# Attention scores of a hybrid decoder block from stacked high and low halves, in fp32r products instead of fp32

## The chip, the core and the metric

The kernel runs on one core of a Trainium2 chip. The time is device time in microseconds (us) of one execution; the profile is one execution of its own, with its own time. TensorE multiplies (PE in the rows, PEld its weight loads), VectorE is DVE, ScalarE is ACT, GpSimd is POOL, and SP is the queue that issues the weight transfers.

## What is computed

A block with 256 tokens and width 1024: an mLSTM mixer and a dense SwiGLU, then attention with three branches (compressed, selected, window) over shared keys and values, then a top-2-of-8 expert SwiGLU, and a last norm. The change touches the scores of the three branches. Sixteen heads of width 64 share four groups of keys. With 256 tokens all four selection blocks are always taken and the window holds everything, so the selected and the window branch differ only in their keys and values.

```python
# cut from nsa_mixer: g groups, r heads in a group
s_c = jnp.einsum('bgrqd,bgcd->bgrqc', qb, k_cmp) * scale - sl5 * dist_c      # 15 compressed keys
p_cmp = safe_softmax(jnp.where(dist_c >= 0, s_c, -jnp.inf))
o_cmp = jnp.einsum('bgrqc,bgcd->bgrqd', p_cmp, v_cmp)
s_s = jnp.einsum('bgrqd,bgqnkd->bgrqnk', qb, ks) * scale - sl6 * dist_s      # selected blocks
o_slc = jnp.einsum('bgrqk,bgqkd->bgrqd', safe_softmax(s_s), vs)
s_w = jnp.einsum('bgrqd,bgkd->bgrqk', qb, kw) * scale - sl5 * dist_w         # window
o_win = jnp.einsum('bgrqk,bgkd->bgrqd', safe_softmax(s_w), vw)
return gb[..., 0:1] * o_cmp + gb[..., 1:2] * o_slc + gb[..., 2:3] * o_win
```

## The kernel before

Five engine programs run side by side, each written out by hand in its own order, and wait for each other through semaphores. There is no scheduler: the order in the code is the order of the work.

**Weights.** All weights come in slots of 1 MB. SP loads them into a ring of 7 (`raw`), each when the slot seven before it has been used (`s_used`). ScalarE rounds a slot to fp32r (`w_hi`, L433), VectorE subtracts (`w_lo`, L853), and TensorE multiplies high by high, low by high and high by low (`mm3`, L1475 to L1477). `split_to(m)` makes the halves up to slot m, on ScalarE and on VectorE; `AHEAD` is 3 slots.

**Ahead of the attention** (about 340 to 407 us). Four slots give the compressed inputs and the two sets of keys: `kt` holds keys with the width of 64 on the rows, twice (rows 0 to 63 and 64 to 127), ScalarE copying the lower groups (L594, L595) and VectorE the upper ones (L1075, L1076). Four slots, with the compression between them, give the queries: bank i holds four heads, and one copy of ScalarE scales and stores it in `qt` (`q_copied`, L604), two heads above each other: even heads on rows 0 to 63, odd ones on rows 64 to 127. The compressed keys go to `kc` in a block form, so that one product serves two heads (L624), and the compressed values to `vbd` (L627), both by ScalarE.

**Attention** (about 407 to 500 us). There are 32 steps, one for a head and a token tile of 128. `ORDER` lists the tile and the group: eight heads of tile 1, eight of tile 0, eight of tile 1, eight of tile 0. A head of tile 1 sees 256 keys in each of two branches, so its score has 512 columns; one of tile 0 sees 128, and has 256. The two are called wide and narrow below. Step n on TensorE is the score of head n+3 (`head_scores`, L1823), one part of the value products of an earlier group (`group_part`, L1849, L1851), and the transposes of head n (`head_transpose`, L1833). Score and value products and transposes are fp32. VectorE adds the position bias to a score out of one of three banks and takes the maximum (L1130, L1134), ScalarE makes the exponentials (L648), VectorE turns the sums into coefficients (L1141, L1142), both scale a half (L675, L1146), TensorE transposes, and ScalarE copies the result for the value products (L656). The compressed scores (`cmp_scores`, L1805) of one tile stand before the loop and those of the other in steps 5 and 6. The first three scores, the first compressed scores and the products of the first value slot stand before the loop, and those of the second value slot follow steps 0 and 1.

**Behind it** come the output projection and the experts, 336 more slots.

These lines of TensorE's program are the ones that the change replaces:

```python
def cmp_scores(t, pairs):
    for pair in pairs:
        ins = mm(B[7][:, pair * 64:pair * 64 + 48], qt[:, pair, cmp_tile(t) * P:(cmp_tile(t) + 1) * P],
                 kc[:, 2 * pair // R, :], start=True, stop=True)
...
    mm(B[n % 3][:, 0:2 * lk], qt[lo:lo + 64, h // 2, t * P:(t + 1) * P], kt[lo:lo + 64, :, h // R, 0:lk],
       start=True, stop=True).then_inc(s_as, 1)
```

## Time and profile before

| | us |
|---|---|
| median of 3 runs | 1437.31 |
| lowest and highest | 1434.43, 1438.07 |
| the profiled execution | 1439.59 |
| its span in the profile | 1437.8 |
| busy in the span: PE, DVE, ACT, POOL | 1391.2, 1184.5, 1022.9, 43.8 |

The profile's page gives the busy time of each engine and, in 40 slices, their shares. The span is the time from the first to the last instruction; the 1.8 us between it and the execution's time lie around it. A matmul's duration in the rows is longer than its distance to the next, since matmuls are pipelined: what one costs is read from start to start, or from the chain of waits, where pieces do not overlap. One fp32 matmul of the program stands as two records in the trace, one fp32r matmul as one. Inputs of type fp32r are printed as f32 as well.

### The profile page before, as it was taken

To read this page: it belongs to the slowest core of one execution; us is meant where nothing else is said; L and a number is where in the kernel's file an instruction comes from. 1 tells how busy PE (TensorE), PEld (TensorE's weight loads), DVE (VectorE), ACT (ScalarE), POOL (GpSimd) and SP (SyncE) were. 2 spreads that over 40 slices of the span, in tenths; PEclk is the share of its full clock that TensorE was granted. 3 is DMA by queue.
4 is the path that set the end of the run, shared out by engine and by line. 5 is a ranking of instruction groups with operands and counts; after the bars stand their busy time and mean duration, and the time that the engine had idled before them with its cause. 6 is when DMAs were issued, how large, how long until landed. Compare 5 with 4: busy or idle time off the path is not lost.

```text
span 1437.8 us, 19005 instructions
## 1 busy us (share of the span) xinstructions
PE 1391.2 (97%) x6962; PEld 1142.7 (79%) x6962; DVE 1184.5 (82%) x1091; ACT 1022.9 (71%) x1066; POOL 43.8 (3%) x98
## 2 busy tenths in 40 slices
PE   7999999999999989999999999999999999999996
PEld 7987888888974578788888878888878888878774
DVE  6846654547768679899999999999999999999997
ACT  5546644435567747788888788887878887887875
POOL 7000000001000010000000000000000000000000
PEclk9999999999999989999999999999999999999999
DMA  7543555554630129899999999999999999999985
GB/s 307 177 162 131 192 189 178 176 203 147 235 118 1 39 94 350 326 394 416 407 399 402 399 391 402 411 395 403 398 388 398 408 409 395 391 401 398 415 353 214
DMA packets 59707, 431.68 MB, mean 300 GB/s; under 512 B 6624, under 2 KB 6624, under 8 KB 7520
## 3 DMA queue, kind: packets, MB, share of 16 engines
q1 hardware_dynamic: 59472, 429.95, 76.8%
q8 instruction: 56, 0.92, 0.2%
q10 hardware_dynamic: 144, 0.52, 0.1%
q14 instruction: 35, 0.29, 0.1%
HBM read 429.40 MB, written 1.05 MB: 299 GB/s over the span
## 4 chain that ended last, share of the span: by engine, by line
PE 89%; DVE 4%; DMA 3%; ACT 2%; issue 1%; POOL 0%; SPq 0%; DVEq 0%; POOLq 0%; ACTq 0%
PE bank L1475 19%; PE bank L1477 19%; PE bank L1476 19%; PE bank L1946 6%; PE bank L1947 6%; PE bank L2008 3%; PE bank L1965 3%; PE bank L1966 3%; DMA raw<-in_moe 3%; PE bank L1823 2%; PE bank L1849 2%; DVE w_lo L1352 1%; PE bank L1917 1%; PE bank L1833 1%; PE bank L1995 1%
## 5 line engine op out<-in xcount | busy, mean ns | idle before, releaser
L1352 DVE TENSOR_TENSOR w_lo<-raw,w_hi 128x2048 fp32r<-128x2048 f32 x332 | 750.6, 2289 | 46.7 <-ACT w_hi L748 44.0
L748 ACT ACTIVATE w_hi<-raw 128x2048 fp32r<-128x2048 f32 x332 | 632.9, 1919 | 137.5 <-DMA raw<-in_moe 58.7
L1475 PE MATMUL bank<-w_hi,ht_hi 128*128 128x512 f32 (+1 forms) x768 | 299.3, 390 | 0.9 <-DVE ht_lo L885 0.9
L1477 PE MATMUL bank<-w_hi,ht_lo 128*128 128x512 f32 (+1 forms) x768 | 296.2, 386 | 0.0
L1476 PE MATMUL bank<-w_lo,ht_hi 128*128 128x512 f32 (+1 forms) x768 | 295.9, 385 | 0.0
L853 DVE TENSOR_TENSOR w_lo<-raw,w_hi 128x2048 fp32r<-128x2048 f32 x73 | 166.6, 2290 | 109.7 <-ACT w_hi L433 109.6
L433 ACT ACTIVATE w_hi<-raw 128x2048 fp32r<-128x2048 f32 x74 | 141.4, 1918 | 96.4 <-PE bank L1477 92.8
L1946 PE MATMUL bank<-w_hi,ht_hi 128*128 128x512 f32 x448 | 177.5, 396 | 1.4 <-DVE w_lo L1352 1.4
L1947 PE MATMUL bank<-w_lo,ht_hi 128*128 128x512 f32 x448 | 174.8, 390 | 0.0
L1475 PEld LDWEIGHTS bank<-w_hi,ht_hi 128*128 128x128 f32 x768 | 144.4, 188 | 29.6 <-issue 1.4
L1477 PEld LDWEIGHTS bank<-w_hi,ht_lo 128*128 128x128 f32 x768 | 144.3, 188 | 29.4
L1476 PEld LDWEIGHTS bank<-w_lo,ht_hi 128*128 128x128 f32 x768 | 144.4, 188 | 28.2
L1475 PE MATMUL bank<-w_hi,at_hi 128*128 128x512 f32 x312 | 122.8, 393 | 2.5 <-DVE w_lo L1352 2.5
L1476 PE MATMUL bank<-w_lo,at_hi 128*128 128x512 f32 x312 | 121.5, 389 | 0.0
L1477 PE MATMUL bank<-w_hi,at_lo 128*128 128x512 f32 x312 | 121.5, 389 | 0.0
L1946 PEld LDWEIGHTS bank<-w_hi,ht_hi 128*128 128x128 f32 x448 | 84.2, 188 | 20.2 <-DVE w_lo L1352 3.1
L1947 PEld LDWEIGHTS bank<-w_lo,ht_hi 128*128 128x128 f32 x448 | 84.2, 188 | 16.9
L1965 PE MATMUL bank<-w_hi,at_b 128*128 128x512 f32 x224 | 91.5, 408 | 3.2 <-DVE w_lo L1352 3.1
L1966 PE MATMUL bank<-w_lo,at_b 128*128 128x512 f32 x224 | 88.7, 396 | 0.0
L1475 PEld LDWEIGHTS bank<-w_hi,at_hi 128*128 128x128 f32 x312 | 58.6, 188 | 17.2 <-DVE w_lo L1352 5.5
L1477 PEld LDWEIGHTS bank<-w_hi,at_lo 128*128 128x128 f32 x312 | 58.6, 188 | 12.3
L1476 PEld LDWEIGHTS bank<-w_lo,at_hi 128*128 128x128 f32 x312 | 58.6, 188 | 11.8
(328 smaller groups left out, 1671.1 us busy)
## 6 DMA issues: line engine op xcount, KB each, us to landing
raw<-in_moe SPq DMA_DIRECT2D x336, 1024.0 KB, 7.8
raw<-in_wts SPq DMA_DIRECT2D x71, 1024.0 KB, 4.9
xs<-in_x SPq DMA_DIRECT2D x2, 512.0 KB, 4.0
out<-xn SPq DMA_DIRECT2D x2, 512.0 KB, 2.6
pk<-in_packed SPq DMA_DIRECT2D x1, 517.0 KB, 5.9
g1b<-in_norm_ffn ACTq DMA_DIRECT2D x1, 512.0 KB, 3.8
gfb<-in_norm_final SPq DMA_DIRECT2D x1, 512.0 KB, 12.0
```

Of the source, the lines that this page charges most:

```text
L433: a(w_hi[:, n % SPLIT, :], raw[:, n % RAW, :], ACT.Copy).then_inc(s_hi, 1)
L748: a(w_hi[:, n % SPLIT, :], raw[:, n % RAW, :], ACT.Copy).then_inc(s_hi, 1)
L853: v.tensor_tensor(w_lo[:, n % RAW, :], raw[:, n % RAW, :], w_hi[:, n % SPLIT, :].bitcast(F32), ALU.subtract).then_inc(s_lo, 1)
L1352: v.tensor_tensor(w_lo[:, n % RAW, :], raw[:, n % RAW, :], w_hi[:, n % SPLIT, :].bitcast(F32), ALU.subtract).then_inc(s_lo, 1)
L1475: mm(out_, sh, mh, start=first, stop=False)
L1476: mm(out_, sh, ml, start=False, stop=False)
L1477: return mm(out_, sl, mh, start=False, stop=last)
L1946: mm(bank[:, :], both, weights(w_hi, n, 512)[:, k, :], start=kk == 0, stop=False)
L1947: ins = mm(bank[:, :], both, weights(w_lo, n, 512)[:, k, :], start=False, stop=kk == 7)
L1965: mm(B[2 + half][:, :], at_b[:, block], weights(w_hi, n, 1024)[:, k, w], start=first, stop=False)
L1966: ins = mm(B[2 + half][:, :], at_b[:, block], weights(w_lo, n, 1024)[:, k, w], start=False, stop=last)
L2008: ins = mm(B[4 + c % 2][:, to:to + CAP_B], src[:, c % 2, j * P:(j + 1) * P], fold[:], start=True, stop=True)
```

## The change

The queries are kept as a high half, rounded to fp32r, and a low half, what the rounding leaves, stacked on the 128 rows: for each head the high half on rows 0 to 63 and the low half on rows 64 to 127 (`q_first` for heads 0 to 7, `q_last` for heads 8 to 15, where `ct` was). The keys' high half `kt_hi` stands twice, as `kt` did, and a product over 128 rows is then (high + low query) times high key. A second and a third product over rows 0 to 63 add the high query times the low key, for each of the two branches (`kt_lo`, eight small tiles in free places). All are fp32r. The compressed scores are built likewise from `kc_hi` and `kc_lo`, for each head instead of each pair.

ScalarE copies each query bank in two halves, and three small copies replace the two of `kc`, two of them to fill a sixteenth column. VectorE makes the low halves of the keys (8 subtractions), of the queries (8) and of the compressed keys (1). GpSimd no longer clears `kc`. The odd buffer of transposed weights (`pt_odd`) and `fold` move to other places.

```diff
@@ ScalarE
-            a(qt[:, 2 * i:2 * i + 2, :], B[i % 2][:, :].rearrange("p (b t) -> p b t", b=2), ACT.Copy,
-              scale=DB ** -0.5).then_inc(s_qc, 1)
+            for odd in range(2):
+                a(queries(i, odd, slice(0, 64)), B[i % 2][64 * odd:64 * odd + 64, :].rearrange("p (b t) -> p b t", b=2), ACT.Copy,
+                  scale=DB ** -0.5).then_inc(s_qc, 1)
...
-        for odd in range(2):
-            rows_ = slice(64 * odd, 64 * odd + 64)
-            a(kc[rows_, :, 32 * odd:32 * odd + NC_], B[5][rows_, 0:G * NC_].rearrange("p (g n) -> p g n", g=G),
-              ACT.Copy).then_inc(s_kc, 1)
+        a(kc_hi[:, :, 0:NC_], B[5][:, 0:G * NC_].rearrange("p (g n) -> p g n", g=G), ACT.Copy).then_inc(s_kc, 1)
+        spare = B[5][:, 0:G].rearrange("p (g o) -> p g o", o=1)
+        a(kc_hi[:, :, NC_:16], spare, ACT.Copy).then_inc(s_kc, 1)
+        a(kc_lo[0:64, :, NC_:16], spare[0:64], ACT.Copy).then_inc(s_kc, 1)
@@ VectorE
+                dve.wait_ge(s_kva, 2 * i + 2)
+                dve.wait_ge(s_kvd, 2 * i + 2)
+                for g in range(G):
+                    rows_ = slice(64 * (g % 2), 64 * (g % 2) + 64)
+                    v.tensor_tensor(kt_lo[i - 2][g][0:64, :], B[4 + i % 2][rows_, (g // 2) * T:(g // 2 + 1) * T],
+                                    kt_hi[rows_, i - 2, g, :].bitcast(F32), ALU.subtract).then_inc(s_kl, 1)
...
+        def q_low(i):
+            for odd in range(2):
+                dve.wait_ge(s_qc, 2 * i + odd + 1)
+                v.scalar_tensor_tensor(queries(i, odd, slice(64, 128)),
+                                       B[i % 2][64 * odd:64 * odd + 64, :].rearrange("p (b t) -> p b t", b=2), DB ** -0.5,
+                                       queries(i, odd, slice(0, 64)).bitcast(F32), ALU.mult, ALU.subtract).then_inc(s_ql, 1)
+
+        for i in range(2):
+            split_to(Q_SLOT[i] + AHEAD)
+            q_low(i)
         split_to(Q_SLOT[2] + AHEAD)
+        q_low(2)
...
+        q_low(3)
+        dve.wait_ge(s_kc, 3)
+        v.tensor_tensor(kc_lo[0:64, :, 0:NC_], B[5][0:64, 0:G * NC_].rearrange("p (g n) -> p g n", g=G),
+                        kc_hi[0:64, :, 0:NC_].bitcast(F32), ALU.subtract).then_inc(s_kcl, 1)
         split_to(BO0 + 1)
@@ TensorE
+            tile = slice(cmp_tile(t) * P, (cmp_tile(t) + 1) * P)
+            for h in heads:
+                to = B[7][:, h * 32:h * 32 + 16]
+                mm(to, query(h)[:, tile], kc_hi[:, h // R, :], start=True, stop=False)
+                ins = mm(to, query(h)[0:64, tile], kc_lo[0:64, h // R, :], start=False, stop=True)
...
-            mm(B[n % 3][:, 0:2 * lk], qt[lo:lo + 64, h // 2, t * P:(t + 1) * P], kt[lo:lo + 64, :, h // R, 0:lk],
-               start=True, stop=True).then_inc(s_as, 1)
+            mm(B[n % 3][:, 0:2 * lk], query(h)[:, tile], kt_hi[:, :, g, 0:lk], start=True, stop=False)
+            for b in range(2):
+                ins = mm(B[n % 3][:, b * lk:(b + 1) * lk], query(h)[0:64, tile], kt_lo[b][g][0:64, 0:lk],
+                         start=False, stop=b == 1)
+            ins.then_inc(s_as, 1)
```

On TensorE, in step 5 of the attention, stand before: the narrow score of head 8, a part of the value products, four pairs of compressed scores and the transposes of head 5.

```order
L1823 MATMUL bank<-kt,qt 128x256
L1849 MATMUL bank<-pt_even,vv 64x512
L1851 MATMUL bank<-pct,vbd 64x128
L1805 MATMUL bank<-kc,qt 128x48 x4
L1833 MATMUL bank<-ident,sc 128x128 x4
```

The same step now; the lines L1848 and L1849 stand eight times each, in turn, of which two pairs are shown at the start.

```order
L1866 MATMUL bank<-kt_hi,q_first 128x256
L1868 MATMUL bank<-kt_lo_113,q_first 128x128
L1868 MATMUL bank<-kt_lo_117,q_first 128x128
L1895 MATMUL bank<-pt_even,vv 64x512
L1897 MATMUL bank<-pct,vbd 64x128
L1848 MATMUL bank<-kc_hi,q_first 128x16
L1849 MATMUL bank<-kc_lo,q_first 128x16
```

One score became three products and the four pairs of compressed scores 16; the transposes (now L1879) still end the step.

On VectorE, from the last splits ahead of the attention to the first bias, stood the gates and then the splits of slots 67 and 68.

```order
L1085 TENSOR_TENSOR gat<-bank,pk 128x2x24 x2
L1091 TENSOR_SCALAR gat<-gat 128x96
L1092 RECIPROCAL gat<-gat 128x96
```

Now the low halves of the last two query banks stand on both sides of the gates, and that of the compressed keys behind them.

```order
L1106 SCALAR_TENSOR_TENSOR q_last<-bank,q_last 64x2x256 x2
L1118 TENSOR_TENSOR gat<-bank,pk 128x2x24 x2
L1124 TENSOR_SCALAR gat<-gat 128x96
L1125 RECIPROCAL gat<-gat 128x96
L1106 SCALAR_TENSOR_TENSOR q_last<-bank,q_last 64x2x256 x2
L1128 TENSOR_TENSOR kc_lo<-bank,kc_hi 64x4x15
```

The splits of slots 67 and 68 follow behind these rows, where before they followed the reciprocal.

## Rows read from the trace of the kernel before

**Rows 1.** PE, PEld, DVE, ACT, POOL busy, PEclk, DMA share, GB/s; page's DMA

```profile
451.00:470.00 19.00, 19.00 (x67) 7.88 (x68) 16.29 (x42) 16.19 (x53) 0.00 (x0) 1.00 0.00 1
522.00:532.00 10.00, 4.69 (x21) 4.24 (x20) 8.83 (x36) 5.70 (x5) 3.06 (x2) 0.52 0.16 67
...
DMA  7543555554630129899999999999999999999985
```

**Rows 2.** Chain of waits in the attention loop: start and length in us

```profile
427.73 0.59 PE bank L1833 x4
432.24 1.02 PE bank L1805 x8
441.69 0.63 PE bank L1823 x2
456.28 1.05 PE bank L1823 x2
```

**Rows 3.** Timeline of DVE: first bias, narrow and wide coefficients

```profile
411.00 0.68 DVE L1130 SCALAR_TENSOR_TENSOR sc<-dat,bank 128x512 f32<-128x512 f32 x1
446.71 0.17 DVE L1141 RECIPROCAL coef<-att 128x2 f32<-128x2 f32 x1
448.31 0.17 DVE L1141 RECIPROCAL coef<-att 128x2 f32<-128x2 f32 x1
463.70 0.17 DVE L1141 RECIPROCAL coef<-att 128x2 f32<-128x2 f32 x1
465.69 0.16 DVE L1141 RECIPROCAL coef<-att 128x2 f32<-128x2 f32 x1
```

**Rows 4.** Timeline of PE: neighbouring fp32r products, 512 and 16 or 8 columns

```profile
330.25 0.39 PE L1477 MATMUL bank<-w_hi,at_lo 128*128 128x512 f32 x1
330.48 0.39 PE L1475 MATMUL bank<-w_hi,at_hi 128*128 128x512 f32 x1
...
519.49 0.26 PE L1899 MATMUL bank<-ws_hi,ht_hi 128*128 128x16 f32 x1
519.60 0.25 PE L1900 MATMUL bank<-ws_hi,ht_lo 128*128 128x8 f32 x1
```

**Rows 5.** Timeline of PE: transposes, 24 fp32r products between, a score

```profile
421.65 0.66 PE L1833 MATMUL bank<-ident,sc 128*128 128x128 f32 x4
...
424.97 1.12 PE L1823 MATMUL bank<-kt,qt 64*128 64x512 f32 x2
```

**Rows 6.** Timeline of PE: first three scores, and the fourth

```profile
406.88 1.98 PE L1823 MATMUL bank<-kt,qt 64*128 64x512 f32 x6 [2.12 <-ACT vbd L627]
...
416.22 1.12 PE L1823 MATMUL bank<-kt,qt 64*128 64x512 f32 x2
```

**Rows 7.** Group of DVE, a query copy of ACT, DVE's waits 352 to 412

```profile
L1153 DVE TENSOR_TENSOR ht_lo<-bank,ht_hi 64x256 fp32r<-64x256 f32 x12 | 4.9, 412 | 1.0 <-ACT ht_hi L664 0.8
...
377.02 0.60 ACT L604 ACTIVATE qt<-bank 128x512 f32<-128x512 f32 x1 [3.35 <-PE bank L1477]
...
DVE w_lo L853 <- ACT w_hi L433: 16.0, 8, 5.2
```

**Rows 8.** Waits 427 to 492: us in total, times, longest

```profile
DVE sc L1130 <- PE bank L1823: 2.9, 5, 0.9
DVE coef L1141 <- ACT sc L648: 1.7, 7, 0.4
DVE pc L1101 <- PE bank L1805: 1.4, 1, 1.4
```

**Rows 9.** ACT and PE: scaling and transposes of heads 20 and 31

```profile
466.31 0.50 ACT L675 ACTIVATE sc<-sc,coef 128x256 f32<-128x256 f32 x1
...
469.13 0.66 PE L1833 MATMUL bank<-ident,sc 128*128 128x128 f32 x4
...
490.87 0.40 ACT L675 ACTIVATE sc<-sc,coef 128x128 f32<-128x128 f32 x1 [0.17 <-DVE coef L1142]
...
491.63 0.44 PE L1833 MATMUL bank<-ident,sc 128*128 128x128 f32 x2
```

More of the change, by code:

```diff
@@ L153, in trunk @@
     assert KD * T * 8 <= (28 + 4) * P * 4
+    ptg = [sb("pt_even", [P, 4, R, P], F32, sg_at)[0], sb("pt_odd", [P, 4, R, P], F32, hk_at + KD * T * 4)[0]]
+    q_last, _ = sb("q_last", [P, 8, T], FR, ct_at)
+    kt_lo = [[sb(f"kt_lo{b}{g}", [P, T], FR, at)[0] for g, at in enumerate(row)]
+             for b, row in enumerate(([xn_at + 4096 + 1024 * g for g in range(4)],
+                                      [sel_at, tri_at, pk_at + 1856, pk_at + 2880]))]
     iot, _ = sb("iot", [P, NE])
@@ L240, in head, with query, queries @@
         return t, R * g + n % R
+    def query(h):
+        return (q_first, q_last)[h // 8][:, h % 8, :]
+    def queries(i, odd, rows):
+        first = 4 * (i % 2) + odd
+        return (q_first, q_last)[i // 2][rows, first:first + 3:2, :]
     def cmp_tile(i):
@@ L1800, in values, with cmp_scores @@
                 ins.then_inc(s_used, 1)
[L1802 to L1807 removed]
+        def cmp_scores(t, heads):
+            tile = slice(cmp_tile(t) * P, (cmp_tile(t) + 1) * P)
[3 more added lines that the diff above has]
+                ins = mm(to, query(h)[0:64, tile], kc_lo[0:64, h // R, :], start=False, stop=True)
+            if heads[-1] == HB - 1:
                 ins.then_inc(s_cs, 1)
```

47 lines of the change are left out of this document (23 added, 24 removed).

## Prediction

> **What bounds the kernel now.** I read the stretches first: between 451 and 470 us, in the middle of the attention, TensorE is busy 19.00 of 19.00 us while VectorE is busy 16.29 and ScalarE 16.19 [rows 1]. TensorE is the bound, but the other two are only 14% below it, so a large saving on TensorE cannot all reach the end. The page's row of DMA tenths [rows 1] says what follows: in the attention the queues are nearly idle (the digits 0, 1, 2), since the ring of 7 weight slots is full, and from the 16th slice on they are full. Loads start again when TensorE frees slots behind the attention, so an earlier end of the attention moves the whole expert part by as much, neither more nor less.
>
> Then the chain of waits, for what a score costs inside the loop: 1.05 us for a head of the later token tile (512 columns, "wide"), 0.63 us for one of the first tile (256 columns, "narrow"), 1.02 us for four pairs of compressed scores [rows 2]. Then VectorE: one wide head takes it 1.99 us (463.70 to 465.69), a narrow one 1.60 us (446.71 to 448.31), both stretches without a wait [rows 3].
>
> **TensorE's part, step by step.** What an fp32r product costs from start to start: with 512 columns 0.23 us, with 16 or 8 columns still 0.11 us [rows 4]. With 256 columns and between fp32 neighbours I take it from a block of 24 such products: from the four transposes at 421.65 to the score at 424.97 are 3.32 us [rows 5], and four transposes before an fp32 score take 0.59 [rows 2], so the block costs 2.73, or 0.114 us each, with what the change from fp32 to fp32r and back costs inside it.
> - Wide score: 0.23 + 2 x 0.114 = 0.46 in place of 1.05, saves 0.59. There are 13 in the loop: 7.7 us.
> - Narrow score: one product of 256 columns and two of 128. No row shows fp32r with 128 columns. Below lies the price of 16 columns (0.11), above that of an fp32 score of 256 columns in two records, 0.63 / 2 = 0.31. I take 0.114, since rows on both sides of 128 columns (16 and 256) show it. 3 x 0.114 = 0.34 in place of 0.63, saves 0.28. There are 16: 4.5 us. At the upper end each would cost 0.74, 0.11 more than now, and the 4.5 saved become 1.8 lost.
> - The first three scores stand together before the loop and take 1.98 us [rows 6], not 3 x 1.05 = 3.15: even heads lie on rows 0 to 63, odd ones on 64 to 127, and two of them overlap. Now 3 x 0.46 = 1.37, saves 0.6.
> - Compressed scores: 8 products of fp32 become 32 of fp32r for each tile. 32 x 0.112 = 3.6 us; now 1.9 before the loop (9.34 us from 406.88 to 416.22, less 1.98 and less 48 x 0.114 for the values [rows 6]) and 2 x 1.02 inside it [rows 2]. Costs 1.7 + 1.55 = 3.3 us.
> TensorE's sum: 7.7 + 4.5 + 0.6 - 3.3 = 9.5 us less work.
>
> A page of the Trainium skill speaks against the change here: "TensorEngine Tiling (Array Packing)", section When to Use Tiling, advises two row tiles where the contraction is 64 deep, and the new score fills all 128 rows. The trace agrees where scores stand together (1.98 us) and only there; in the loop a transpose stands between any two. By that rule all scores of before would count half, the saving would be gone, and TensorE's work would rise.
>
> **Ahead of the attention.** VectorE gets 8 subtractions of 64x256 for the keys at 0.41 us (the same form in the attention [rows 7]), 8 of 64x512 for the queries at up to 0.69 (by the biased score, 512 elements read from a bank [rows 3]) and a small one: 3.3 + 5.5 + 0.3 = 9.1 us. In 352 to 412 us it waits 16.0 us for ScalarE's high halves [rows 7], and these additions fall between those waits; w_lo of a slot is made about one slot ahead of its use. Cost 0; if that cover were gone, at most 9.1. ScalarE copies each query bank in two halves, so 0.60 more for each of four [rows 7]; it waits for TensorE before each. Behind the last, one more small copy stands in front of the vbd copies, for which TensorE waits 2.12 us before its first score [rows 6]. Its price lies between 0 and 0.60 (a copy of 512 columns); I take 0.25, as it has 4 to 60 columns. TensorE's added waits (for the low halves of keys and queries) stand before products 10 us and more behind them; the one for kc_lo is met while ScalarE still copies vbd. The split of slot 67 moves behind the queries, and slot 68 is still the last thing before VectorE's first bias at 411.00 [rows 3].
>
> **What becomes late next.** The opening gets no faster: 0.25 later, 0.6 saved, 1.7 more for the compressed scores, so the fourth score, 416.22 now [rows 6], starts at about 417.6, and wins it back only over the next three heads. At the two heads with compressed scores TensorE again needs 1.55 us more and saves 0.6; the compressed bias, which waited 1.4 us for it [rows 8], comes some 0.45 us later.
>
> From there to the end VectorE and ScalarE set the pace. The 8 wide scores of the second half lie in 451 to 470: TensorE's 19.00 us become 19.00 - 8 x 0.59 = 14.3, under the 16.29 of VectorE and the 16.19 of ScalarE [rows 1]. In the middle TensorE trails: the scaling of head 20 starts at 466.31 and takes 0.50, its transposes start at 469.13, 2.3 us behind readiness [rows 9]. But for the last head this slack is almost gone: scaled at 490.87 + 0.40 = 491.27, transposed at 491.63, 0.36 us [rows 9]. The loop ends earlier by that 0.36 and by what the chain of VectorE and ScalarE gains itself. It gains its waits for TensorE: 2.9 us for scores from 427 us on, and of the 1.7 us for the exponentials some part, as ScalarE waited for transposes in its turn [rows 8]; I take half, 0.85. Sum: 0.36 + 2.9 + 0.85 - 0.45 - 0.25 = **3.4 us**. Of 9.5 us saved on TensorE 6.1 become waits. Lower end: the 0.85 is 0 and every second of the five waits is replaced by one for ScalarE: 1.5. Upper end: all 1.7, and the compressed bias not late: 4.7; I say 5. Behind the loop nothing changes.
>
> The profiled execution took 1439.59 us (span 1437.8), 2.3 above the median of the runs, 1437.31. It would come to 1436.2, the median to 1433.9.
>
> **Rivals.**
> - *TensorE's saving arrives whole.* Then the last transposes would not be held by their scaling, and the time is 1437.3 - 9.5 = 1427.8. For it: TensorE is 100% busy and trails by 2.3 us in the middle. Against: 0.36 us at the last head [rows 9], 16.29 of 19.00 on VectorE.
> - *Nothing arrives.* Short fp32r products are dear: at the upper end for 128 columns TensorE saves 9.5 - 16 x 0.39 = 3.3 us, and the narrow heads, for which VectorE needs only 1.60 us [rows 3] and TensorE sets the pace, take back what the wide ones give: about 0, 1437. Against: no row shows a short fp32r product over 0.12 us at full clock [rows 4].
> - *Slower: the clock falls inside the loop.* TensorE would now stop at nearly every head. In 522 to 532 it was busy 4.69 of 10 us and its granted clock was 0.52 [rows 1], so near the 1.2 GHz level and not the 2.4. Ten microseconds at half clock in the loop make 9 us of work into 18; less some 4 us of slack and with the gain of 3.4 given back in part, about +5: 1442. [...] Against: even with 6.1 us of new waits in 80 TensorE stays over 90% busy, and in 451 to 470 the clock is 1.00 [rows 1]. The Trainium skill's page "TensorE: Matmul & The Clock Gate", section What's actually happening, has the throttled state as the default that activity releases; that is this rival's rule, and the row of 522 to 532 agrees with it.
>
> **How the numbers follow.** A measurement of this kernel tells about 0.3%, 4.3 us, from no change. Forecast 0.57 (1432.3 to 1435.8; about a fifth of it gains over 4.3), whole saving or most of it 0.17, nothing arrives 0.16, clock or a lost cover ahead of the attention 0.10. Faster by over 0.3%: 0.17 + 0.12 = 0.29; slower 0.10; within 0.3%: 0.61. The range leaves out the outer half of the whole saving and of the slower case: 1429 to 1440.
>
> **What would show it.** In the profile of the changed kernel a wide score should be three products in 0.46 us, a narrow one in 0.34, and the compressed scores 16 times 0.11 in a row. VectorE's wait for scores should be nearly gone from 427 us on, TensorE should show idle before the transposes of some 6 us in sum, ended by ScalarE's or VectorE's scaling, and the last transposes should start 3 us earlier against the first score. Ahead of the attention no product should wait for w_lo, xc_lo or the new low halves. I am wrong if narrow scores take over 0.5 us, if TensorE still shows no idle time in the loop (then the first rival holds), if VectorE's heads become longer than 1.99 and 1.60 us, or if the granted clock in the loop falls below 1.00.

## The result and the profile after

The changed kernel takes 1452.06 us (median of 4 runs, 1449.89 to 1454.80) beside 1436.94 for the kernel before: a ratio of 1.0103, 95% interval 1.0087 to 1.0118. It is slower by 15.1 us, where 1433.9 and a range of 1429 to 1440 were forecast. Its profiled execution has a span of 1453.0 us.

First the stretches of the changed kernel. The columns are start and end, length, then busy time (and instructions) of PE, PEld, DVE, ACT and POOL, the granted clock of TensorE, the DMA share and GB/s:

```profile
407.00:411.00 4.00, 2.19 (x8) 1.19 (x8) 3.38 (x4) 3.60 (x8) 0.00 (x0) 1.00 0.61 244
411.00:421.00 10.00, 10.00 (x35) 9.13 (x34) 7.04 (x13) 4.08 (x14) 0.00 (x0) 0.53 0.00 1
421.00:425.00 4.00, 4.00 (x19) 3.98 (x20) 0.00 (x0) 0.00 (x0) 0.00 (x0) 0.50 0.00 0
425.00:444.00 19.00, 18.42 (x130) 15.46 (x129) 12.60 (x34) 10.21 (x30) 0.00 (x0) 0.99 0.33 111
444.00:447.00 3.00, 3.00 (x14) 2.72 (x15) 1.54 (x6) 1.25 (x5) 0.00 (x0) 0.80 0.00 0
447.00:459.00 12.00, 12.00 (x36) 8.73 (x37) 3.51 (x11) 3.61 (x13) 0.00 (x0) 0.50 0.01 1
462.00:509.00 47.00, 46.39 (x215) 25.58 (x212) 41.14 (x126) 41.94 (x147) 0.00 (x0) 1.00 0.00 1
```

Where the kernel before had the full clock without a break from 402 to 516 us (the stretch of rows 1 is a piece of that), this one falls to the 1.2 GHz level twice, over 411 to 425 and over 447 to 459 us. In both TensorE is listed as busy for all of the time. From 447 to 459 us VectorE and ScalarE have little to do: 3.51 and 3.61 us of work in 12.

What TensorE does at the two falls, from its timeline (start, length, line, output and inputs with rows x columns, count). L1866 and L1868 are the new score's high and low products, L1848 and L1849 those of the compressed scores, L1512 to L1514 the value projection, L1895 and L1897 a part of the value products, L1879 the transposes of a head (a transpose stands as one record):

```profile
408.81 0.50 PE L1866 MATMUL bank<-kt_hi,q_first 128*128 128x512 f32 x1 [1.86 <-ACT vbd L642]
409.24 0.50 PE L1868 MATMUL bank<-kt_lo,q_first 64*128 64x256 f32 x2
...
411.39 0.28 PE L1848 MATMUL bank<-kc_hi,q_first 128*128 128x16 f32 x1
411.60 0.32 PE L1849 MATMUL bank<-kc_lo,q_first 64*128 64x16 f32 x1
411.85 0.38 PE L1848 MATMUL bank<-kc_hi,q_first 128*128 128x16 f32 x1
...
413.08 0.38 PE L1848 MATMUL bank<-kc_hi,q_first 128*128 128x16 f32 x1
413.39 0.38 PE L1849 MATMUL bank<-kc_lo,q_first 64*128 64x16 f32 x1
...
421.14 0.58 PE L1512 MATMUL bank<-w_hi,hk_hi 128*128 128x256 f32 x1
...
421.52 0.41 PE L1513 MATMUL bank<-w_lo,hk_hi 128*128 128x256 f32 x1
421.74 0.41 PE L1514 MATMUL bank<-w_hi,hk_lo 128*128 128x256 f32 x1
...
428.66 0.40 PE L1866 MATMUL bank<-kt_hi,q_first 128*128 128x512 f32 x1
428.98 0.50 PE L1868 MATMUL bank<-kt_lo,q_first 64*128 64x256 f32 x2
429.42 0.66 PE L1879 MATMUL bank<-ident,sc 128*128 128x128 f32 x4
```

and at the first head with compressed scores in the loop:

```profile
443.23 0.28 PE L1848 MATMUL bank<-kc_hi,q_first 128*128 128x16 f32 x1
443.44 0.27 PE L1849 MATMUL bank<-kc_lo,q_first 64*128 64x16 f32 x1
443.64 0.28 PE L1848 MATMUL bank<-kc_hi,q_first 128*128 128x16 f32 x1
...
446.84 1.11 PE L1879 MATMUL bank<-ident,sc 128*128 128x128 f32 x4
```

A product of 16 columns starts 0.205 us after the one before it at full clock (443.23, 443.44, 443.64), and 0.31 at half clock (413.08, 413.39). The forecast had 0.112. The 32 of the first tile take from 411.39 to 421.14, 9.75 us, where 3.6 were forecast. Behind them the value projection runs at some 0.21 per product (421.52, 421.74) for another 4 us, twice its price at full clock, and the fourth score starts at 428.66, where the kernel before had it at 416.22 [rows 6].

The 32 products of the first tile lengthen the stretch at half clock, but they did not begin it. The first of them starts at 411.39, and the clock is down a third of a microsecond later, when one or two of them have run:

```profile
411.50:411.75 0.25, 0.25 (x2) 0.23 (x2) 0.25 (x1) 0.00 (x0) 0.00 (x0) 0.87 0.00 0
```

What stands in front are TensorE's stop of 1.86 us and 2.58 us of the new scores. The experiments come back to this.

The effect on the other engines, from the waits in 430 to 492 us (total, times, longest):

```profile
DVE sc L1167 <- PE bank L1868: 16.5, 5, 11.2
DVE pc L1138 <- PE bank L1849: 6.4, 1, 6.4
```

These are VectorE's waits for scores and for compressed scores, 2.9 and 1.4 us before [rows 8].

To place the 15 us I cut the attention at the transposes of heads 0, 8 and 31, in this and in all later kernels. Times in us; "clock" is where the granted clock was under 0.9 between 402 and 516 us, in steps of 3 us.

| kernel | first score to head 0 | heads 0 to 8 | heads 8 to 31 | span | clock under 0.9 |
|---|---|---|---|---|---|
| before | 10.39 | 23.98 | 50.38 | 1437.8 | nowhere |
| changed | 20.61 | 32.75 | 46.22 | 1453.0 | 411-426, 444-459 |
| low_rows128_compressed | 17.33 | 25.87 | 46.22 | 1438.8 | 411-423, 444-450 |
| low_rows128_all | 15.98 | 31.47 | 45.82 | 1444.5 | 408-420, 435-456 |
| compressed_fp32 | 17.42 | 24.25 | 46.23 | 1440.5 | 411-423 |
| compressed_one_product | 14.02 | 22.51 | 46.38 | 1431.2 | 408-417 |
| compressed_one_spread | 12.50 | 22.61 | 46.79 | 1431.8 | 408-414 |
| one_product_rows128_low | 12.42 | 25.12 | 46.76 | 1434.6 | 408-417, 432-441 |
| one_spread_rows128_low | 11.01 | 21.85 | 47.17 | 1432.3 | 411-414 |
| one_spread_scores_first | 10.90 | 22.62 | 46.79 | 1428.8 | nowhere |
| after_wide_columns | 27.17 | 38.77 | 48.47 | 1464.3 | 411-432, 456-480 |

The changed kernel is 10.2 us longer ahead of head 0, 8.8 longer over heads 0 to 8, and 4.2 shorter over heads 8 to 31. So the loop's gain is there, where the compressed scores are done, and both losses lie in the two stretches that hold the compressed scores. Its first score starts 1.9 us later than before (408.81 against 406.88), but the products ahead of any changed instruction are 2.2 us later already, and in the kernels below (one_spread_scores_first apart, where this code is changed) the start of the first score varies between 406.7 and 410.0 with nearly the same code in front of it. So it is not laid to the change. What follows head 31 takes 940.5 to 946.2 us in all the traces, so a sum of one trace holds to some 3 us.

### The profile page after: what moved, and what is told of

The parts are those of the page before. It is cut to its first block, busy times and chain, and to the rows that moved or that the text cites. A ratio compares the mean times of both kernels' runs of the same rounds, so it can differ in the third digit from the quotient of the medians.

```text
span 1453.0 us, 19158 instructions
## 1 busy us (share of the span) xinstructions
PE 1406.0 (97%) x7026; PEld 1165.6 (80%) x7026; DVE 1192.6 (82%) x1108; ACT 1023.0 (70%) x1071; POOL 43.7 (3%) x97
## 3 DMA queue, kind: packets, MB, share of 16 engines
HBM read 429.40 MB, written 1.05 MB: 296 GB/s over the span
## 4 chain that ended last, share of the span: by engine, by line
PE 88%; DVE 5%; ACT 2%; DMA 2%; issue 1%; POOL 0%; SPq 0%; DVEq 0%; POOLq 0%; ACTq 0%
PE bank L1512 19%; PE bank L1514 19%; PE bank L1513 19%; PE bank L1993 6%; PE bank L1994 6%; PE bank L2012 3%; PE bank L2013 3%; PE bank L2055 3%; DMA raw<-in_moe 2%; DVE w_lo L1389 2%; PE bank L1895 1%; PE bank L1964 1%; PE bank L1879 1%; PE bank L2042 1%; PE bank L1868 1%
## 5 line engine op out<-in xcount | busy, mean ns | idle before, releaser
L1512 PE MATMUL bank<-w_hi,ht_hi 128*128 128x512 f32 (+1 forms) x768 | 299.4, 390 | 1.1 <-DVE ht_lo L900 0.9
L1514 PE MATMUL bank<-w_hi,ht_lo 128*128 128x512 f32 (+1 forms) x768 | 296.3, 386 | 0.0
L1512 PEld LDWEIGHTS bank<-w_hi,ht_hi 128*128 128x128 f32 x768 | 144.4, 188 | 29.9 <-issue 1.4
L1514 PEld LDWEIGHTS bank<-w_hi,ht_lo 128*128 128x128 f32 x768 | 144.3, 188 | 29.5
L1512 PE MATMUL bank<-w_hi,at_hi 128*128 128x512 f32 x312 | 122.8, 394 | 3.0 <-DVE w_lo L1389 3.0
L1514 PE MATMUL bank<-w_hi,at_lo 128*128 128x512 f32 x312 | 121.5, 389 | 0.0
L1512 PEld LDWEIGHTS bank<-w_hi,at_hi 128*128 128x128 f32 x312 | 58.5, 188 | 17.9 <-DVE w_lo L1389 6.2
L1514 PEld LDWEIGHTS bank<-w_hi,at_lo 128*128 128x128 f32 x312 | 58.6, 188 | 12.4
```

The lines of the kernel that those rows point to most:

```text
L1512: mm(out_, sh, mh, start=first, stop=False)
L1514: return mm(out_, sl, mh, start=False, stop=last)
```

## Experiments

Three theories stood after this, and the expectations go by their letters. **A**: changing between products over 128 and over 64 rows costs TensorE about 0.09 us at each change, and this is the loss. **B**: an fp32r product of 16 columns costs 0.2 us whatever its rows. **C**: the clock falls because the products have few columns, whatever rows they use, and that is most of the loss.

### Taking the change of rows out

low_rows128_compressed: the compressed low-key product uses all 128 rows.

```
...
-        v.tensor_tensor(kc_lo[0:64, :, 0:NC_], B[5][0:64, 0:G * NC_]...
+        v.tensor_tensor(kc_lo[:, :, 0:NC_], B[5][:, 0:G * NC_]...
...
-                ins = mm(to, query(h)[0:64, tile], kc_lo[0:64, h // R, :], start=False, stop=True)
+                ins = mm(to, query(h)[:, tile], kc_lo[:, h // R, :], start=False, stop=True)
```

> The changed kernel with one edit: the second product of each compressed score runs over all 128 rows (the compressed keys' low half stands twice, so it also adds low query times low key) instead of rows 0 to 63. The count of products stays 32 for each tile. Theory A (a product pays its weight load in the open when its rows differ from those of the one before): start to start of the compressed products falls from 0.205 us at full clock (0.31 at half) to 0.11, so the 32 before the loop take 3.6 us instead of 9.8, and the time comes down by some 10 to 12 us, to 1440 to 1442. Rival B (a 16-column fp32r product costs 0.2 us whatever its rows): distance and time stay as in the changed kernel, 1452. Rival C (the clock falls because the products have few columns, and that is most of the loss): the distance falls to 0.11 but the clock still falls behind 411 us, and the time is 1446 or more.

low_rows128_all: the same, and the attention's low-key products too (the low keys are written to rows 64 to 127 as well, 8 more subtractions).

```
+                    for half in range(2):
+                        v.tensor_tensor(kt_lo[i - 2][g][64 * half:64 * half + 64, :], ...
...
-                ins = mm(B[n % 3][:, b * lk:(b + 1) * lk], query(h)[0:64, tile], kt_lo[b][g][0:64, 0:lk],
+                ins = mm(B[n % 3][:, b * lk:(b + 1) * lk], query(h)[:, tile], kt_lo[b][g][:, 0:lk],
```

> As low_rows128_compressed, and the two low-key products of each attention score run over 128 rows too; for that VectorE makes each of the eight low key tiles on both halves, 8 more subtractions of 0.41 us ahead of the attention. Theory A: a wide score with the transposes behind it comes down from 1.24 to about 1.05 us on TensorE, a narrow one from 0.85 to 0.65, some 6 us less work on TensorE in the loop, of which perhaps 3 arrive, since the last heads already wait for their scaling: 1437 to 1439. Rival B: no difference to low_rows128_compressed. If the added VectorE work ahead of the attention is on the path, products ahead of 409 us wait for w_lo and the time is longer by up to 3 us.

Measured: 1442.01 us (4 runs, ratio to before 1.0043, 1.0027 to 1.0060) and 1446.13 (4 runs, 1.0068, 1.0051 to 1.0084). Timeline of TensorE in the first:

```profile
410.57 0.26 PE L1849 MATMUL bank<-kc_lo,q_first 128*128 128x16 f32 x1
410.68 0.26 PE L1848 MATMUL bank<-kc_hi,q_first 128*128 128x16 f32 x1
```

and in the second:

```profile
408.32 0.40 PE L1869 MATMUL bank<-kt_lo,q_first 128*128 128x256 f32 x2
408.56 0.39 PE L1867 MATMUL bank<-kt_hi,q_first 128*128 128x512 f32 x1
408.79 0.39 PE L1869 MATMUL bank<-kt_lo,q_first 128*128 128x256 f32 x2
```

The compressed products are back at 0.11 us, and a wide score at 0.46 to 0.47 (408.32 to 408.79), the two prices of the forecast. So the change of rows is what they lacked, and B is out: it takes a pair of compressed products from 0.22 to 0.41 and a wide score from 0.46 to 0.86. Each product of a pair starts some 0.205 us behind the other, the one over 64 rows like the one over 128, so the price lies in the change in either direction and not in the 64 rows. Of the 15.1 us, 10.0 come back with the first edit by the medians (8.6 by the ratios to the kernel before). Its time is at the upper end of what A gave it, and the clock still falls, as C had it, though the time stays under C's 1446.

The second edit missed its expectation of 1437 to 1439 by 7 us. With less work on TensorE in the loop the clock stays down from 438 to 453 us, and the kernel takes 4.1 us more than the first (1445.57 to 1448.31 against 1440.57 to 1445.39). Granted clock of low_rows128_all, same columns as above, and a product just behind a stop of TensorE:

```profile
420.00:435.00 15.00, 14.34 (x120) 13.92 (x120) 9.87 (x26) 6.91 (x20) 0.00 (x0) 1.00 0.39 137
438.00:453.00 15.00, 15.00 (x57) 11.34 (x55) 5.76 (x20) 5.36 (x19) 0.00 (x0) 0.50 0.00 1
...
436.33 1.58 PE L1896 MATMUL bank<-pt_even,vv 128*64 128x512 f32 x2 [1.05 <-ACT pt_even L671]
```

TensorE had stopped for 0.66 us up to 434.34 and for 1.05 up to 436.33. The two value products behind the second stop are partly slow already (1.58 us; two take 1.07 at full clock), and the first compressed product of the loop starts only at 438.28. Here the clock fell right behind the stops, ahead of the compressed products.

In the opening, too, the clock of this kernel is down before its first compressed product starts:

```profile
409.25:409.50 0.25, 0.25 (x3) 0.25 (x2) 0.07 (x1) 0.25 (x1) 0.00 (x0) 0.79 0.08 33
...
409.53 0.21 PE L1849 MATMUL bank<-kc_hi,q_first 128*128 128x16 f32 x1
```

### 32 products added to the kernel before

The kernel before with 32 added fp32r products, whose results nobody reads, ahead of its own compressed scores; rows and columns varied.

```
+        for j in range(32):
+            r_ = slice(0, 64 if j % 2 else P)     # or slice(0, P)
+            mm(B[7][:, 0:16], hk_hi[r_, j % KD, 0:P], hk_lo[r_, j % KD, 0:16], start=True, stop=True)
         cmp_scores(0, range(HB // 2))
```

> The kernel before with 32 added fp32r products of 16 columns ahead of the first compressed scores; they go to a bank that is written anew behind them, and alternate between 128 and 64 rows. It measures the disputed product by itself, 128 columns of stationary, 16 columns moving. Theory A: 0.205 us each at full clock, 6.6 us in sum if the clock holds. Rival B: the same here and in before_32_full_rows. Rival C: the clock falls during or behind them here and in before_32_full_rows.

> As before_32_alternating, but all 32 added products have 128 rows. Theory A: 0.11 us each, 3.6 us in sum, clock 1.00. Rival B: 0.2 us each. Rival C: the clock falls in spite of the shorter run.

> before_32_full_rows with 256 columns in each of the 32 added products instead of 16. By start to start they should cost the same, 0.11 us each, 3.7 us. If it is the few columns that let the clock fall behind 413 us, it stays at 1.00 here and the time is about 3.7 above before, 1440. If any such burst behind the idle time before the scores does it, the clock falls as there, to 0.50 for some 7 us.

> The kernel before with 32 added fp32r products of 256 columns ahead of the compressed scores, over 128 and 64 rows in turn: the fourth of a table of two by two (16 or 256 columns, all rows or alternating). If both few columns and the alternation let the clock fall, each by itself, it falls to 0.50 here as in after_wide_columns, the 32 take 0.205 us each at first and 0.255 at half clock (7 to 8 us), and the time is 1437 + 7.5 + 3 to 6 = 1447 to 1451. If the fall in after_wide_columns came from the scores in front of the products (fp32r, also alternating) and not from the products, the clock holds at 1.00 here: 6.6 us for the 32, and 1443 to 1445.

One run each. Per product is start to start at full clock; the fall is the first 3-us window under 0.9:

| | time, us | per product | clock |
|---|---|---|---|
| 16 columns, all rows | 1441.66 | 0.112 | falls in 414-417, back at 423 |
| 16 columns, rows alternating | 1448.42 | 0.206 | falls in 411-414, back at 423 |
| 256 columns, all rows | 1443.64 | 0.123 | 1.00 throughout |
| 256 columns, rows alternating | 1454.2 | 0.315 | falls in 414-417, back at 432 |

The prices come from the timeline of TensorE, a group's length less the last record over the count less one. In before_32_alternating:

```profile
408.94 1.30 PE L1862 MATMUL bank<-hk_lo,hk_hi 128*128 128x16 f32 x6
```

and in before_32_alternating_wide:

```profile
411.64 1.64 PE L1862 MATMUL bank<-hk_lo,hk_hi 128*128 128x256 f32 x5
```

that is (1.30 - 0.27) / 5 = 0.206 and (1.64 - 0.38) / 4 = 0.315. The stretch 414 to 417 us of before_32_full_rows (columns as above):

```profile
414.00:417.00 3.00, 3.00 (x16) 3.00 (x16) 2.82 (x9) 2.02 (x8) 0.00 (x0) 0.52 0.00 0
```

of before_32_wide_columns:

```profile
414.00:417.00 3.00, 3.00 (x29) 3.00 (x28) 2.90 (x7) 1.82 (x6) 0.00 (x0) 1.00 0.00 0
```

and of before_32_alternating_wide:

```profile
414.00:417.00 3.00, 3.00 (x7) 1.73 (x7) 2.82 (x9) 2.02 (x9) 0.00 (x0) 0.53 0.00 0
```

Theory A's price is confirmed in the other kernel, and on the clock each theory had half. In these four traces the clock fell behind 16 columns on all rows, where A expected 1.00, and behind 256 columns with the rows changing, and did not fall behind 256 columns on all rows. All four stretches show TensorE fully busy in the profile, so the busy share doesn't tell them apart. The last was forecast too low (0.205 to 0.255 us a product, and 1447 to 1451 in all), and so was the time of the third (1440). The last was run because the next experiment had come out against its expectation.

Two limits belong to this table. Each row is one trace, and in all four the added products stand behind the same stop of TensorE (2.13 us) and the same old scores; no such row was run without the stop. And the fall comes 4 us and more behind the first added product (at about 413 where that starts at 408.94, at about 414 where it starts at 409.75 and 409.77), not a third of a microsecond as in the changed kernel.

after_wide_columns: the changed kernel, each compressed product over 256 columns of the score keys; it leaves out the compressed keys, so its compressed scores are not those of the block.

```
+                to = B[7][:, 0:256]
-                mm(to, query(h)[:, tile], kc_hi[:, h // R, :], start=True, stop=False)
-                ins = mm(to, query(h)[0:64, tile], kc_lo[0:64, h // R, :], start=False, stop=True)
+                mm(to, query(h)[:, tile], kt_hi[:, 0, h // R, 0:256], start=True, stop=False)
+                ins = mm(to, query(h)[0:64, tile], kt_lo[0][h // R][0:64, 0:256], start=False, stop=True)
```

> The changed kernel, with each of its 64 compressed products over 256 columns instead of 16: the score keys' halves (kt_hi, kt_lo of tile 0) stand in for the compressed keys, so the compressed scores and what is worked out from them are wrong; count and rows of the products (128 and 64 in turn) are those of the changed kernel. If it is the few columns of these products that let the granted clock fall, the clock holds at 1.00 through steps 5 and 6 and nearly so from 408 to 426 us, a pair of products still takes 0.41 to 0.43 us (the alternation), the stretch before the loop takes 6.6 to 7 us instead of 9.8, head 0 is transposed 6 to 7 us earlier than in the changed kernel, and the time is 1452 - 10 to 14 = 1438 to 1442. If the alternation of rows itself is what lets the clock fall, the clock is 0.50 over about 10 us as in the changed kernel and the time stays at 1450 to 1454.

It took 1466.11 us (4 runs, 1.0193, 1.0166 to 1.0219), 14 us more than the changed kernel, where 10 to 14 less were expected if few columns were the whole reason. Its timeline:

```profile
412.90 0.58 PE L1849 MATMUL bank<-kt_hi,q_first 128*128 128x256 f32 x1
413.41 0.58 PE L1850 MATMUL bank<-kt_lo,q_first 64*128 64x256 f32 x1
```

One product starts 0.51 us after another, with the rows changing and at half clock. The expectation was also wrong in the price of a change: it put a pair at 0.41 to 0.43, which is what two products of 16 columns take. A change costs more with longer products: 0.09 us with 16 columns, 0.19 with 256.

### Shorter compressed scores

compressed_one_product: the keys' high and low halves stand side by side, so one product of 32 columns on all 128 rows does a head, and VectorE adds the two halves of the result (one more step for each tile).

```
-    kc_hi, _ = sb("kc_hi", [P, G, 16], FR)
-    kc_lo, _ = sb("kc_lo", [P, G, 16], FR)
+    kc2, _ = sb("kc2", [P, G, 32], FR)
+    kc_hi, kc_lo = kc2[:, :, 0:16], kc2[:, :, 16:32]
...
+                ins = mm(to, query(h)[:, tile], kc2[:, h // R, :], start=True, stop=True)
...
+            step(v.tensor_tensor(p, both[:, :, 16:16 + NC_], p, ALU.add))
```

> low_rows128_compressed with the two products of a compressed score joined into one of 32 columns (high keys beside low keys, VectorE adds the two column sets, one more step of 0.4 us for each tile): 16 products for a tile in place of 32, all over 128 rows. Attention scores as in the changed kernel. Theory A with the clock as second cause (few columns in a row let the clock fall): before the loop 1.8 us of 32-column products in place of 3.6, so the clock either holds or falls for less long; at steps 5 and 6 0.9 us each, where it should hold. Time 1434 to 1438. If the clock falls as in low_rows128_compressed (0.50 for 8 to 10 us behind 411), the number of short products is not what decides, and the time is 1439 or more.

compressed_one_spread: the same 16 products of the first tile stand one by one behind three value products each, those of the second in five small pieces.

```
+                if i == 0:
+                    cmp_scores(0, (8 * t + k,))
...
-                cmp_scores(1, range(8 * (n - 5), 8 * (n - 5) + 8))
+                cmp_scores(1, range(4) if n == 5 else range(11, 14))
...
```

> compressed_one_product with the 16 products of the first tile spread among the value products (one behind each three of 256 columns) and those of the other tile in three pieces within steps 5 and 6. Same work, other order. If the clock falls because short products stand in a row, it holds here, at 1.00 from 405 to 500 us, and the time is 1431 to 1434, below before. If it falls as in compressed_one_product, the cause is the attention scores or the idle time before them, not the compressed products.

compressed_fp32: one fp32 product of 16 columns over the stacked halves, with the compressed keys kept in fp32 and no low half of them.

```
...
+                ins = mm(to, query(h)[:, tile].bitcast(F32), kc_hi[:, h // R, :], start=True, stop=True)
```

> The changed kernel's attention scores, but the compressed scores in fp32: one product for each head over the stacked halves, 16 columns, no low keys, no change of rows. 16 fp32 products for a tile, 32 records of 0.12 us as in the kernel before, so 3.8 us in place of 1.9 before and 9.8 in the change. It is the attention scores' half of the change, and its compressed part is 2 us dearer a tile than before. If few columns let the clock fall, whatever the type, it falls here as in low_rows128_compressed and the time is 1440 to 1443. If fp32r is what does it, the clock holds: 1435 to 1438.

Measured, 10 runs each: compressed_one_product 1433.05 (0.9976, 0.9965 to 0.9987), compressed_one_spread 1434.17 (0.9978, 0.9965 to 0.9992) and compressed_fp32 1440.81 (1.0023, 1.0011 to 1.0035). Stretches of compressed_one_product:

```profile
409.00:415.00 6.00, 6.00 (x30) 5.86 (x31) 5.83 (x10) 2.26 (x8) 0.00 (x0) 0.55 0.00 1
420.00:443.00 23.00, 22.42 (x143) 16.84 (x143) 19.07 (x55) 15.90 (x49) 0.00 (x0) 1.00 0.26 92
```

With the new attention scores untouched and only the compressed ones rewritten, 19.0 us come back against the changed kernel by the medians (18.2 by the ratios), and the result is below the kernel before. In the loop the clock holds. In the opening it still falls for a few microseconds, with 16 short products where there were 32. The fp32 form holds the clock in the loop too, where each half of its 16 products takes 1.96 us. In the opening the halves take 2.83 and 3.42 (411.62, 414.45 and 417.87 are their starts and their end), and the clock is down from 411 to 423: 7.0 us more than before from the first score to head 0. Its time is the one expected if the clock falls whatever the type. Spreading the products shortens the opening by 1.5 us in the trace and shows in no time (the two intervals coincide).

The spread kernel missed its expectation that the clock holds, and what was written for that case applies: the cause of the opening's fall is then "the attention scores or the idle time before them, not the compressed products". In all the kernels with the new scores and a stop of 1.8 us or more in front of them, the clock goes down 1.2 to 3.3 us behind the start of the first score. In the changed kernel, compressed_one_product and compressed_one_spread, which have the same stop and the same scores, it is 2.9 to 3.0 us in all three. What the form of the compressed scores sets there is how long the clock stays down: about 14, 7 and 3 us.

### Taking the change of rows out of the attention's scores as well

one_product_rows128_low and one_spread_rows128_low: the two kernels above with the attention's low-key product on all 128 rows (the diff of low_rows128_all).

> The kernel compressed_one_product, with the attention's low-key product over all 128 rows too, which takes the row change out of every score (8 more subtractions on VectorE ahead of the attention). If a row change costs 0.09 to 0.10 us at each side of a low-key product, a wide head saves 0.37 us and a narrow one 0.25 in TensorE's row (13 x 0.37 + 16 x 0.25 = 8.8), of which the loop, paced by VectorE and ScalarE at most heads, gives 1 to 3: 1430 to 1432. If the shorter scores let the granted clock fall in the loop, as they did in low_rows128_all (0.50 from 438 to 453 us), 5 or more are lost: 1436 to 1440.

> The kernel compressed_one_spread, with the attention's low-key product over all 128 rows. As one_product_rows128_low: 1430 to 1433 if only the row changes go; 1436 to 1440 if the clock falls. If the clock falls in one_product_rows128_low and not here, what lets it fall is the compressed products in a row, and the spread cures it; if it falls in both, the short scores themselves do.

Measured, 12 runs each: 1437.80 (1.0008, 0.9993 to 1.0023) and 1434.09 (0.9977, 0.9967 to 0.9987). The clock falls in the first, over 432 to 441 us, and not in the loop of the second. In the opening it falls in both, and in the second before its first compressed product starts:

```profile
411.00:412.00 1.00, 1.00 (x7) 0.92 (x7) 0.41 (x2) 0.90 (x1) 0.00 (x0) 0.61 0.04 16
...
412.38 0.23 PE L1853 MATMUL bank<-kc,q_first 128*128 128x32 f32 x1
```

Timeline of the first where it falls in the loop:

```profile
433.08 1.59 PE L1897 MATMUL bank<-pt_even,vv 128*64 128x512 f32 x2 [1.05 <-ACT pt_even L671]
...
435.02 1.89 PE L1851 MATMUL bank<-kc,q_first 128*128 128x32 f32 x8
```

TensorE had stopped for 0.78 and 1.05 us just before, where compressed_one_product with its longer scores has one stop of 0.58. The products at 433.08 are partly slow already (1.59 us where two take 1.07), so the fall came right behind the stops and not at the eight short products that follow. That corrects what the expectation offered: the spread did not simply cure a row of short products. Why the clock held in the spread kernel, whose stops are 0.78 and 1.04 us, isn't settled by this pair. One trace doesn't speak for every execution here: the 12 of one_product_rows128_low lie between 1432.30 us, with a mean granted clock of 0.988 over the whole kernel, and 1442.81 with 0.983.

The second kernel answers what the cheaper scores are worth where the clock holds. TensorE's work over heads 8 to 31 is 3 us less, the time is the same, and heads 8 to 31 take 47.17 us, not less than 46.79. The stretch of those heads in one_spread_rows128_low:

```profile
443.00:490.00 47.00, 42.35 (x208) 24.32 (x208) 42.08 (x129) 42.32 (x150) 0.00 (x0) 1.00 0.00 1
```

and in one_spread_scores_first (below), whose scores change rows:

```profile
439.00:485.00 46.00, 45.28 (x206) 24.82 (x205) 41.25 (x127) 41.27 (x147) 0.00 (x0) 1.00 0.01 1
```

42.35 of 47 us busy against 45.28 of 46: what TensorE saved became waits. In the later half ScalarE has no room left, as this stretch of one_spread_rows128_low shows:

```profile
473.00:483.00 10.00, 9.67 (x49) 5.42 (x48) 8.93 (x29) 9.95 (x35) 0.00 (x0) 1.00 0.01 2
```

### Filling the stop in front of the first score

one_spread_scores_first: compressed_one_spread, with the wait for the compressed keys moved behind the first three scores, which don't use them.

```
-        pe.wait_ge(s_kc, 7)
-        pe.wait_ge(s_kcl, 1)
...
         for n in range(3):
             head_scores(n)
+        pe.wait_ge(s_kc, 7)
+        pe.wait_ge(s_kcl, 1)
```

> The kernel compressed_one_spread, with the wait for the compressed keys moved behind the first three scores, which don't use them. TensorE's stop of 1.86 us ahead of the first score goes, or is filled by 2.6 us of scores: the first score starts 1.8 us earlier against the last hidden product in front of it, and so does all of the attention: 1434.2 - 1.9 = 1432.3 by this. If the stop of 1.86 us is part of what lets the clock fall at 410 us (0.84 and 0.59 in two windows of 3 us in compressed_one_spread), the clock holds and another 1 to 1.5 us come: 1431. If the scores wait for something else that ends as late (the query halves), nothing moves: 1434.

Measured: 1430.77 us (5 runs, 0.9963, 0.9950 to 0.9977), the fastest of all, and faster than both kernels of this study. Its timeline:

```profile
405.01 0.47 PE L1867 MATMUL bank<-kt_hi,q_first 128*128 128x512 f32 x1 [0.85 <-issue]
...
408.02 0.18 PE L1850 MATMUL bank<-kc,q_first 128*128 128x32 f32 x1
```

The stop of 1.86 us is 0.85, and the clock stays at 1.00 from 402 to 516 us. The stretch from first score to head 0 is 1.6 us shorter than in compressed_one_spread with the same products in it, so that is the clock. The stop gave 1.0 and not the 1.9 expected. Together they make 2.6, where the medians differ by 3.4 and the ratios by 2.2. The products in front of the stop and behind it are the same in both kernels, so the stop is part of what led to the opening's fall; it is one pair of traces. In the kernel before the clock held behind a stop of 2.12 us, with the old scores. Why it falls with the new ones is open.

## Why the prediction was wrong

- **The step that failed is the compressed scores' term, 32 x 0.112 = 3.6 us for each tile.** 0.11 was read from two products that both use all 128 rows [rows 4]; the changed kernel alternates 128 and 64. A product then costs 0.205, at full clock 6.6 us a tile. The first tile took 9.75 us and the second 3.6 + 5.0, together 18.4. The extra over the forecast's 7.2 is 11.2: 5.9 by the change of rows (64 x 0.093) and 5.2 by the clock. low_rows128_compressed shows the price, before_32_alternating shows it in the other kernel.
- **The clock.** The main forecast left the clock at 1.00, and the slower rival, at a chance of 0.10 with a lost cover, had it fall at the wrong places. It let the clock fall at stops throughout the loop, and weighed against it that TensorE stays over 90% busy. In the changed kernel it fell in the opening, a third of a microsecond into the compressed scores, and again during those of step 5, in stretches where TensorE is listed as 100% busy, and it stayed at 1.00 over heads 8 to 31. The rival's stops were not beside the point, though: in low_rows128_all and one_product_rows128_low the loop's fall came right behind stops, and the opening's fall went when its stop was shortened. Its price by the traces: 3.2 and 2.0 us on the compressed products, 2.0 on the value projection behind them (421.14 to 428.66 are 7.5 us, 48 x 0.114 are 5.5), and 3.4 on the transposes, scores and value parts of heads 5 to 7, taken as what heads 0 to 8 are longer than in compressed_one_product (10.2) without what the compressed products explain (8.6 - 1.8). Together 10.6 us, beside 5.9 for the change of rows: 16.5 us lost, less what the loop gains. Both are worked out from traces. The medians say that 19.0 us hang on the form of the compressed scores, with the time that the clock is down among them. What began the opening's fall is not settled.
- **A rule read and not weighed.** The Trainium skill's page "TensorEngine Tiling (Array Packing)", section Tiling Modes, Key Properties, states "Mode switching requires drain". The forecast took from that page the advice against filling 128 rows and passed over this one, which meets the change at every product. The traces agree with it in that each change costs time: 0.205 against 0.112 us, and 0.315 against 0.123 with 256 columns. The page gives no price.
- **Wide scores, forecast 0.46 in place of 1.05.** The score takes 0.83 to 0.86 us (408.81 to 409.67). But the transposes in front of it take 0.41, not 0.59 (486.35 to 486.76 below). Some 0.1 of that is again the change of rows, which the kernel before had at every score, from transposes on 128 rows to a score on 64: in front of other transposes on 128 rows four took 0.49 there (427.66 to 428.15). Together 1.24 in place of 1.64: 0.40 saved, not 0.59. The 0.46 holds without the change of rows.
- **Narrow scores, forecast 0.34 in place of 0.63.** They take 0.65, above the 0.5 named as the sign of being wrong; with 0.17 less for the transposes in front, 0.15 is saved and not 0.28. The bound taken from 16 and 256 columns held for the column count and missed the rows.

```profile
486.35 0.65 PE L1879 MATMUL bank<-ident,sc 128*128 128x128 f32 x4
486.76 0.36 PE L1866 MATMUL bank<-kt_hi,q_last 128*128 128x256 f32 x1
487.05 0.43 PE L1868 MATMUL bank<-kt_lo,q_last 64*128 64x128 f32 x2
487.41 0.64 PE L1895 MATMUL bank<-pt_even,vv 128*64 128x512 f32 x1
```

- **First three scores, forecast 1.37 in place of 1.98.** 2.58 (408.81 to 411.39): they cost 0.6 where 0.6 was to be saved. The overlap of row tiles in the kernel before is worth more than the new form here.
- **Ahead of the attention, forecast 0 for VectorE and 0.25 for the added small copy.** The first was right within what a trace tells: no product waits for a low half. The 0.25 did not come: TensorE's stop for vbd is 1.86 us where it was 2.12 [rows 6].
- **What arrives, forecast 3.4 us.** Heads 8 to 31 took 4.2 us less, and in the kernels without the fall another 1.4 over heads 0 to 8. The size is near, the way to it was not: TensorE's saving in the loop was 13 x 0.40 + 16 x 0.15 = 7.6 us and not 12.2, TensorE still was busy 46.39 of 47 us (462 to 509), and 5.6 of the smaller saving arrived. The limit by VectorE and ScalarE lies just behind it: one_spread_rows128_low took 3 us more off TensorE and nothing arrived. The last transposes of the changed kernel were held by the scaling, as forecast:

```profile
508.39 0.44 PE L1879 MATMUL bank<-ident,sc 128*128 128x128 f32 x2 [0.61 <-ACT sc L690]
```

- **The new attention scores alone** were a gain: with compressed scores of one product a head the kernel takes 1433.05 us, within 1 us of the 1433.9 forecast. That is luck: it comes of a smaller saving and a cheaper compressed part, not of the forecast's terms.

## What to carry to other kernels

Read the price of a short product from a row whose neighbours use the rows of the array as its neighbours will in the new kernel. Where a change makes products alternate between 128 and 64 rows, count every change (0.09 us with 16 columns, 0.19 with 256), or make the short operand as tall as the other. Where a long row of short or alternating products is put in, or a stop moves in front of new products, price the work behind it at half clock too, and look at the granted clock of the stretch and not at its busy share. Before a fall is laid to the products in it, look in narrow stretches at what ran when it began. Halves that lie side by side in one product, with an addition on another engine, were the cheaper form here.

## What the runs showed of the hardware

- A change between 128 and 64 rows takes a product of 16 columns from 0.112 to 0.206 us and one of 256 columns from 0.123 to 0.315, start to start at full clock; 0.31 and 0.51 at half clock.
- The granted clock fell to 0.50 while the profile listed TensorE as busy for the whole stretch (10.00 of 10.00 us, clock 0.53). Of the kernel before with 32 added products, it fell with 16 columns on all rows and with 256 columns on alternating rows, and not with 256 columns on all rows, all behind a stop of 2.13 us. In the changed kernel it stayed at 0.50 through 4 us of dense products of 256 columns (421 to 425 us).
- With the new scores behind a stop of 1.86 us the clock was down 0.3 us into the compressed scores in the changed kernel, and before the first of them in low_rows128_all and one_spread_rows128_low. With the stop at 0.85 us it held.
- Less work on TensorE can cost time: low_rows128_all took 4.1 us more than low_rows128_compressed, with 0.50 granted from 438 to 453 us, and one_product_rows128_low 4.8 us more than compressed_one_product. In both the loop's fall came behind stops of some 0.7 and 1.05 us.
- Four fp32 transposes took 0.41 us in front of an fp32r product on 128 rows, 0.49 in front of fp32 transposes on 128 rows, and 0.59 in front of an fp32 score on 64 rows [rows 2].
- Left open: why the clock held in the loop of one_spread_rows128_low and fell in that of one_product_rows128_low. The two differ in where eight short products stand; each has one trace, and the fall began ahead of those products. Open too: why the clock fell with the new scores behind a stop, and held with the old ones behind a longer one.
